# Gate/up products of three dense layers: high and low tokens in one product of 512 columns

## The chip, the cores and the metric

One core of a Trainium2 chip. The time is device microseconds of one execution. The kernel before takes 2243.74 us, the median of 3 runs (2243.52 to 2244.27).

## What is computed

One batch of 256 tokens, width 1,024, goes through four layers in fp32. Layers 0 and 1 are a first block (attention, a layer norm, a feed-forward part; layer 1's is a mixture of 8 experts), layers 2 and 3 a second one (a gated delta rule beside a local attention, then a feed-forward part with a convolution over the tokens). The change touches the feed-forward part of layers 0, 2 and 3:

```python
def swiglu(x, w_gate, w_up, w_down):            # layer 0, inner width 3584
    return (jax.nn.silu(x @ w_gate) * (x @ w_up)) @ w_down
# layers 2 and 3, inner width 2816: h = x @ ffn_up is convolved over the tokens (3 taps and a bias,
# per channel), its gate half goes through gelu, is multiplied by the other half, then @ ffn_down
```

## The kernel before

Every matrix product is done in three products of rounded numbers (type fp32r): a weight w is split into w_hi (w rounded) and w_lo = w - w_hi, and the tokens in the same way. `mm3` (line 787) then adds hi*hi, hi*lo and lo*hi into one PSUM bank.

**Weights.** They come in units of 128x2048 (1 MB), in the order of `stream_order`. SP loads them into six slots `raw`, one after the other. `split_hi` (line 519) on the scalar engine casts a unit into one of three places `w_hi`; `split_lo` (line 529) on the vector engine subtracts into `w_lo`. The unit that goes into a place waits until the products that read the place before have ended. `walk(key)` (through `ahead`, line 535) stands in both engines' programs and splits the unit three behind `key`. All orders are written out by hand, in each engine's own queue.

**A dense stage** (`dense_ffn`, line 986) has n steps: 14 in layer 0, 11 in layers 2 and 3. A step s makes 256 gate and 256 up channels. `gate_up(s)` reads two units, the first and the last four of the eight 128-row chunks of x. For each unit, each half (gate, up), each m (128 channels of the half) and each chunk kc there are three products: weights 128x128 stationary, 256 tokens moving, out 128x256. Gate fills bank 4 + 2 (s % 2), up the bank after it, so the steps take turns with two pairs of banks. `down(s)` multiplies the hidden tile of the step with unit ("dn", s) into banks 0 to 3: 24 products of 512 columns. The order on the matmul engine is

```
gate_up(0), then for s = 0 .. n-4: gate_up(s+1), down(s)
then gate_up(n-2), gate_up(n-1), down(n-3),
then for each tile of tokens t: down(n-2, t), down(n-1, t)
```

`down(s)` waits for `hidden` of s, the last operation of `split_hidden` (line 2116: a cast and a subtraction, both 128x512, on the vector engine).

**Behind a step.** Layer 0: the scalar engine takes silu of the gate bank (line 1544), the vector engine multiplies with the up bank (line 2081) and splits the result. Layers 2 and 3: for each half the scalar engine writes the last tap and the bias from the bank (line 1556, two instructions of 128x256), then the vector engine adds the other two taps, again from the bank (lines 2096 and 2101, two instructions each). Then gelu (`gelu`, line 1565), the product with the up half (`gated_mul`, line 2110) and `split_hidden`. The scalar queue of a step is: split for walk("gu", s, 0), the taps of both halves, split for walk("gu", s, 1), gelu, split for walk("dn", s-1). The vector queue is: split, convolution of gate, convolution of up, split, multiply, hidden split, split.

`features` (line 826) makes these products and also those of the input projections of layers 2 and 3. `open_bank` (line 750) waits on the matmul engine until the reader of a bank's former contents is done.

Of the kernel before, what the change touches and what calls it, by code (L numbers as in the profile page):

```python
# [28 lines left out]
P = 128  # L29
S = 256  # L30
# [196 lines left out]
def build_program(nc, A, plan, debug=None):  # L227
    cst_np, cst_at = constants()
    NC = cst_np.shape[1]
    with ExitStack() as ctx:  # L230
# [65 lines left out]
        local_tmp = arena[:, 1024:1536].rearrange("p (a b c) -> p a b c", a=4, b=16)  # L296
        ffn = carve(0, [("sg", (2, 2, S)), ("cbg", (2, 2, S)), ("cbv", (2, 2, S)), ("gg", (2, 2, S)), ("h", (2, 2, S))])
        moe = carve(0, [("sel", (NT, P)), ("lgT", (S,)), ("more", (NT, NE, NE)), ("even", (NT, NE, NE)), ("sg", (2, 512)),
# [450 lines left out]
        def _(pe):  # L749
# [75 lines left out]

            def features(o, key_a, key_b, cols, name_a, names_b, units=range(2), stage=None):

                for i, key in ((i, (key_a, key_b)[i]) for i in units):
                    if stage:
                        for t in range(NT):  # L830
                            tile_ready(stage, t, (i,))
                    u = unit(M, pe, key)
                    for half in range(2):
                        for m in range(2):
                            for kc in range(4 * i, 4 * i + 4):
                                c0 = (kc % 4) * 512 + cols(half, m)
                                mm = mm3(o[half][:, m * S:(m + 1) * S], [w[:, c0:c0 + P] for w in u],
                                         [a[:, kc, :] for a in xT], kc == 0 and m == 0, kc == KC - 1, lone=False)
                        if i == 1:
                            mm.then_inc(*M.groups.mark(*names_b[half]))  # L840
                    if i == 0:
                        mm.then_inc(*M.groups.mark(*name_a))
                        released(M, unit_at[key], *name_a)
                    else:
                        released(M, unit_at[key], *names_b[1])
# [140 lines left out]
            def dense_ffn(L):  # L986
                n = FFN_STEPS[L]

                def gate_up(s):
                    o = [open_bank(M, 4 + 2 * (s % 2) + half) for half in range(2)]  # L990
                    features(o, ("gu", L, s, 0), ("gu", L, s, 1), lambda half, m: half * 256 + m * P,
                             ("unit", "gu", L, s, 0), [("gu", L, s, 0), ("gu", L, s, 1)],
                             stage=None if s else (L, "mix"))

# [132 lines left out]
            def delta(L):  # L1127
# [20 lines left out]
                def project(nb, b0, units=range(2)):  # L1148
                    features([bank[b0 + j] for j in range(2)], ("in", L, 2 * nb), ("in", L, 2 * nb + 1),
                             lambda j, m: (2 * j + m) * P, ("unit", "in", L, 2 * nb),  # L1150
                             [("cv", L, 2 * nb), ("cv", L, 2 * nb + 1)], units)
# [237 lines left out]
        def _(ac):  # L1389
# [135 lines left out]
            def half_squares(L, which, t, halves):  # L1525
# [7 lines left out]
                root(L, which, t, ss[:, t, 0:1], 1.0 / DM, C("rms_eps"))  # L1533

            def dense_act(L):
                n = FFN_STEPS[L]
                for s in range(n):
                    b = 4 + 2 * (s % 2)
                    walk("gu", L, s, 0)
                    if L == 0:  # L1540
                        ac.wait_ge(*M.groups.at("gu", L, s, 0))
                        if s >= 2:
                            ac.wait_ge(*hidden.at(L, s - 2))
                        nc.scalar.activation(ffn["sg"][:, s % 2, :, :].rearrange("p a b -> p (a b)"), bank[b][:, :], ACT.Silu) \
                            .then_inc(*M.free[b].mark("sg", L, s))
                        walk("gu", L, s, 1)
# [18 lines left out]
            def gelu(L, s):  # L1565
                ac.wait_ge(*M.free[4 + 2 * (s % 2)].at("cb", L, s, 0))
                nc.scalar.activation(ffn["gg"][:, s % 2, :, :].rearrange("p a b -> p (a b)"),
# [296 lines left out]
        def _(ve):  # L1864
# [197 lines left out]
            def pre_turned(L, which, t):  # L2062
# [3 lines left out]
                for g in range(2):  # L2066
# [4 lines left out]
                        .then_inc(*M.free[b].mark("xT", (L, which), t, g))  # L2071

            def dense_dve(L):
                n = FFN_STEPS[L]
                for s in range(n):
                    b = 4 + 2 * (s % 2)
                    walk("gu", L, s, 0)
                    if L == 0:
                        ve.wait_ge(*M.free[b].at("sg", L, s))
                        ve.wait_ge(*M.groups.at("gu", L, s, 1))  # L2080
                        V_.tensor_tensor(ffn["h"][:, s % 2, :, :].rearrange("p a b -> p (a b)"),
                                         ffn["sg"][:, s % 2, :, :].rearrange("p a b -> p (a b)"), bank[b + 1][:, :], ALU.mult) \
                            .then_inc(*M.free[b + 1].mark("h", L, s))
                        walk("gu", L, s, 1)
                        ve.wait_ge(*M.free[b + 1].at("h", L, s))
                        split_hidden(L, s)
# [3 lines left out]
                    for half, buf in enumerate((ffn["cbg"], ffn["cbv"])):  # L2090
                        ve.wait_ge(*M.groups.at("gu", L, s, half))
                        ve.wait_ge(*M.act.at("tap", L, s, half))
                        o = bank[b + half]
                        for m in range(2):
                            c = half * 22 + 2 * s + m
                            step(V_.scalar_tensor_tensor(buf[:, s % 2, m, 1:S], o[:, m * S:m * S + S - 1], fcw[:, c, 1:2],
                                                         buf[:, s % 2, m, 1:S], ALU.mult, ALU.add))
                        sync()
                        for m in range(2):
                            c = half * 22 + 2 * s + m  # L2100
                            ins = V_.scalar_tensor_tensor(buf[:, s % 2, m, 2:S], o[:, m * S:m * S + S - 2], fcw[:, c, 0:1],
                                                          buf[:, s % 2, m, 2:S], ALU.mult, ALU.add)
                        ins.then_inc(*M.free[b + half].mark("cb", L, s, half))
                    walk("gu", L, s, 1)
# [5 lines left out]
            def gated_mul(L, s):  # L2110
                ve.wait_ge(*M.act.at("gelu", L, s))
                ve.wait_ge(*M.free[5 + 2 * (s % 2)].at("cb", L, s, 1))
                chain(V_.tensor_tensor(ffn["h"][:, s % 2, :, :], ffn["gg"][:, s % 2, :, :], ffn["cbv"][:, s % 2, :, :], ALU.mult))
# [610 lines left out]
```

## Time and profile before

| | |
|---|---|
| median of 3 runs | 2243.74 us |
| profiled execution | 2243.76 us, span of its trace 2242.0 us |
| matmul engine (PE) busy | 2177.8 us, 97%, 12,316 products |
| weight loads (PEld) busy | 1864.8 us, 83% |
| vector engine (DVE) busy | 1699.2 us, 76% |
| scalar engine (ACT) busy | 1389.8 us, 62% |
| mean granted clock | 0.992 of full |

PE is the matmul engine, PEld its weight loads, which run beside products. The length of a product includes its way through the pipeline, so products overlap in the rows: what one costs is the distance to the start of the next. "[0.91 <-ACT ...]" is idle time ahead of an instruction and what ended it. L790 is the one line in `mm3` that issues every product of the three-product kind.

### The profile page before, as it was taken

Reading aid. Unit: us, or ns where it says so; the run is one execution under the profiler, and the core shown is the slowest. Engines: PE = TensorE matmul, PEld = TensorE weight load, DVE = VectorE, ACT = ScalarE, POOL = GpSimd, SP = SyncE. Lnnn points to the kernel's source line nnn. Section 1 sums busy time; section 2 is a strip of 40 time slices with the busy share of each in tenths; the row PEclk is TensorE's granted clock in tenths of the full one; section 3 lists DMA queues with packets and bytes.
Section 4 is the critical chain, followed back from the end, with each engine's and each line's share of the span. In section 5 each row is a group of like instructions: output and inputs, shape, how many; then the busy total and the mean of one; then the engine's idle time right before and its main releaser. Section 6 shows DMA issues by size and latency. Waiting matters only on the chain.

```text
span 2242.0 us, 32331 instructions
## 1 busy us (share of the span) xinstructions
PE 2177.8 (97%) x12316; PEld 1864.8 (83%) x12316; DVE 1699.2 (76%) x1876; ACT 1389.8 (62%) x1470; POOL 54.9 (2%) x72
## 2 busy tenths in 40 slices
PE   8899999889999999999999999989999999999998
PEld 6699997668888888888888887769979998988998
DVE  6745457768888888888888889867677777776766
ACT  5543334747777777777777777656465446565444
POOL 2000000010000000000000003000000000000000
PEclk9999999999999999999999999999999999999999
DMA  9655555359999999999999999844135554233551
GB/s 385 230 196 184 185 182 183 117 181 384 369 388 374 382 374 379 378 374 383 367 386 369 392 360 393 338 157 151 66 124 206 178 188 146 93 123 141 180 190 55
DMA packets 82234, 573.35 MB, mean 256 GB/s; under 512 B 9603, under 2 KB 9715, under 8 KB 16803
## 3 DMA queue, kind: packets, MB, share of 16 engines
q1 hardware_dynamic: 76752, 545.82, 64.4%
q0 software_dynamic: 5376, 26.12, 3.2%
q8 instruction: 70, 1.15, 0.2%
q14 instruction: 36, 0.27, 0.0%
HBM read 564.03 MB, written 17.83 MB: 260 GB/s over the span
## 4 chain that ended last, share of the span: by engine, by line
PE 86%; ACT 5%; DVE 5%; issue 2%; DMA 1%; SPq 0%; ACTq 0%; POOL 0%; DVEq 0%
PE bank L790 79%; ACT w_hi L527 2%; DVE w_lo L532 2%; PE bank L1095 1%; ACT arena L1430 1%; PE bank L1220 1%; PE bank L1230 1%; PE bank L1135 1%; DVE R L1937 0%; ACT L527 0%; PE bank L872 0%; PE bank L864 0%; DMA raw<-in_wu_qkv 0%; DVE arena L1950 0%; PE bank L765 0%
## 5 line engine op out<-in xcount | busy, mean ns | idle before, releaser
L532 DVE TENSOR_TENSOR w_lo<-raw,w_hi 128x2048 fp32r<-128x2048 f32 x506 | 1159.1, 2301 | 348.9 <-ACT w_hi L527 347.3
L527 ACT CAST w_hi<-raw 128x2048 fp32r<-128x2048 f32 x506 | 965.7, 1911 | 456.3 <-PE bank L790 453.6
L790 PE MATMUL bank<-w_hi,xT_hi 128*128 128x512 f32 x1184 | 472.4, 399 | 16.0 <-DVE w_lo L532 5.4
L790 PE MATMUL bank<-w_hi,xT_lo 128*128 128x512 f32 x1184 | 464.5, 392 | 0.0
L790 PE MATMUL bank<-w_lo,xT_hi 128*128 128x512 f32 x1184 | 464.1, 392 | 0.0
L790 PE MATMUL bank<-xT_hi,w_hi 128*128 128x256 f32 x1344 | 381.5, 284 | 7.1 <-DVE w_lo L532 3.9
L790 PE MATMUL bank<-xT_lo,w_hi 128*128 128x256 f32 x1344 | 381.0, 283 | 0.0
L790 PE MATMUL bank<-xT_hi,w_lo 128*128 128x256 f32 x1344 | 381.0, 283 | 0.0
L790 PE MATMUL bank<-w_hi,aT_hi 128*128 128x512 f32 x864 | 343.8, 398 | 3.2 <-DVE w_lo L532 3.2
L790 PE MATMUL bank<-w_lo,aT_hi 128*128 128x512 f32 x864 | 336.9, 390 | 0.0
L790 PE MATMUL bank<-w_hi,aT_lo 128*128 128x512 f32 x864 | 336.8, 390 | 0.0
L790 PEld LDWEIGHTS bank<-w_hi,xT_hi 128*128 128x128 f32 x1184 | 224.0, 189 | 75.5 <-DVE w_lo L532 13.8
L790 PEld LDWEIGHTS bank<-xT_hi,w_hi 128*128 128x128 f32 x1344 | 258.5, 192 | 8.9 <-issue 7.7
L790 PEld LDWEIGHTS bank<-w_hi,xT_lo 128*128 128x128 f32 x1184 | 224.0, 189 | 48.2
L790 PEld LDWEIGHTS bank<-w_lo,xT_hi 128*128 128x128 f32 x1184 | 224.5, 190 | 44.4 <-issue 0.2
L790 PEld LDWEIGHTS bank<-xT_lo,w_hi 128*128 128x128 f32 x1344 | 258.6, 192 | 1.1
L790 PEld LDWEIGHTS bank<-xT_hi,w_lo 128*128 128x128 f32 x1344 | 258.6, 192 | 0.0
L790 PEld LDWEIGHTS bank<-w_hi,aT_hi 128*128 128x128 f32 x864 | 162.4, 188 | 37.4 <-DVE w_lo L532 4.8
L790 PEld LDWEIGHTS bank<-w_hi,aT_lo 128*128 128x128 f32 x864 | 162.2, 188 | 35.1
L790 PEld LDWEIGHTS bank<-w_lo,aT_hi 128*128 128x128 f32 x864 | 162.6, 188 | 30.4
L1556 ACT ACTIVATE arena<-bank,fcw 128x256 f32<-128x256 f32 x88 | 44.9, 560 | 61.3 <-PE bank L790 61.3
L1592 ACT ACTIVATE arena<-bank 128x512 f32<-128x512 f32 x56 | 33.6, 600 | 42.7 <-PE bank L790 42.6
(334 smaller groups left out, 1610.1 us busy)
## 6 DMA issues: line engine op xcount, KB each, us to landing
raw<-in_wu_eg SPq DMA_DIRECT2D x112, 1024.0 KB, 7.0
raw<-in_wu_eu SPq DMA_DIRECT2D x112, 1024.0 KB, 7.1
raw<-in_wu_ed SPq DMA_DIRECT2D x112, 1024.0 KB, 7.3
raw<-in_wu_up SPq DMA_DIRECT2D x44, 1024.0 KB, 4.8
raw<-in_wu_ffn_gu SPq DMA_DIRECT2D x28, 1024.0 KB, 4.9
raw<-in_wu_in SPq DMA_DIRECT2D x28, 1024.0 KB, 4.8
raw<-in_wu_down SPq DMA_DIRECT2D x22, 1024.0 KB, 4.9
raw<-in_wu_ffn_d SPq DMA_DIRECT2D x14, 1024.0 KB, 4.9
```

The costliest lines, as they stand in the source:

```text
L527: nc.scalar.copy(w_hi[:, place(i), :], src).then_inc(*E.hi.mark("unit", i))
L532: nc.vector.tensor_tensor(w_lo[:, place(i), :], raw[:, i % RAW, :], w_hi[:, place(i), :].bitcast(F32), ALU.subtract) \
L790: mm = nc.tensor.matmul(o, l[i], r[j], start=(first and n == 0), stop=(last and n == 2), skip_group_check=not lone)
L1095: mm = nc.tensor.transpose(o[:, c * P:(c + 1) * P], moe["h"][:, f % 2, c * P:(c + 1) * P], ident)
L1135: return lambda dst, h: nc.tensor.matmul(dst, lhs(h), rhs(h), start=True, stop=True)
L1220: of_level(n, "X", t, t, lambda dst, i: nc.tensor.matmul(dst, dn["LT"][:, i, :], dn["D"][:, i, :], start=True, stop=True))
L1230: of_level(n, "D", t, 2 + t, lambda dst, i: nc.tensor.matmul(dst, dn["DT"][:, i, :], dn["Xl"][:, i, :], start=True, stop=True))
L1430: ins = nc.scalar.activation(att["pr"][:, i, e, a:b], att["s"][:, i, e, a:b], ACT.Exp, bias=nmax[:, i, e, q:q + 1], scale=-1.0, accum_out= ...
L1556: ins = nc.scalar.activation(buf[:, s % 2, m, :], bank[b + half][:, m * S:(m + 1) * S], ACT.Identity, bias=fcw[:, c, 3:4], scale=fcw[:, c, ...
L1592: nc.scalar.activation(moe["sg"][:, f % 2, :], bank[b][:, :], ACT.Silu).then_inc(*E.free[b].mark(tag, "sg", f))
```

## The change

The high and low parts of x^T become one tensor, the parts 8 KB apart in a partition. `features` of the dense layers now makes two products for a chunk where it made three: w_hi stationary with 512 moving columns (256 high, 256 low) into a whole bank, and w_lo with the 256 high columns into the second half of the same bank. Each (half, m) has a bank of its own, 4 + 2 half + m, so a step fills four banks, and every step the same four. The first half of a bank then holds hi*hi, the second the corrections; they are added afterwards: the scalar engine copies the second half to SBUF (`corrections`), the vector engine adds it to the first (`sum_half`), and everything behind reads the sum from SBUF. The input projections keep the old function under the name `features_in`. The order of steps, units and splits stays.

```diff
-        xT = [sb(f"xT_{part}", [P, KC, S], F32R) for part in ("hi", "lo")]
+        x_both = sb("xT", [P, 2, KC, S], F32R)
+        xT = [x_both[:, part, :, :] for part in range(2)]
...
+            def features(L, s, stage=None):
+
+                for i in range(2):
+                    key = ("gu", L, s, i)
...
+                    u = unit(M, pe, key)
+                    for half in range(2):
+                        for m in range(2):
+                            b = 4 + 2 * half + m
+                            o = open_bank(M, b) if i == 0 else bank[b]
+                            both = o[:, :].rearrange("p (a n) -> p a n", a=2)
+                            for kc in range(4 * i, 4 * i + 4):
+                                c0 = (kc % 4) * 512 + half * 256 + m * P
+                                nc.tensor.matmul(both, u[0][:, c0:c0 + P], x_both[:, :, kc, :], start=(kc == 0), stop=False,
+                                                 skip_group_check=True)
+                                mm = nc.tensor.matmul(o[:, S:2 * S], u[1][:, c0:c0 + P], xT[0][:, kc, :], start=False,
+                                                      stop=(kc == KC - 1), skip_group_check=True)
+                        if i == 1:
+                            mm.then_inc(*M.groups.mark("gu", L, s, half))
...
+            def corrections(L, s, half):
+                ac.wait_ge(*M.groups.at("gu", L, s, half))
+                if s:
+                    for m in range(2):
+                        ac.wait_ge(*M.free[4 + 2 * half + m].at("sum", L, s - 1))
+                for m in range(2):
+                    ins = nc.scalar.copy(ffn["cor"][:, half, m, :], bank[4 + 2 * half + m][:, S:2 * S])
+                ins.then_inc(*M.act.mark("cor", L, s, half))
+
+            def summed(L, s, half):
+                for m in range(2):
+                    ac.wait_ge(*M.free[4 + 2 * half + m].at("sum", L, s))
...
                     if L == 0:
-                        ac.wait_ge(*M.groups.at("gu", L, s, 0))
+                        corrections(L, s, 0)
+                        corrections(L, s, 1)
+                        summed(L, s, 0)
...
                     for half, buf in enumerate((ffn["cbg"], ffn["cbv"])):
-                        ac.wait_ge(*M.groups.at("gu", L, s, half))
+                        corrections(L, s, half)
+                        summed(L, s, half)
                         for m in range(2):
                             c = half * 22 + 2 * s + m
-                            ins = nc.scalar.activation(buf[:, s % 2, m, :], bank[b + half][:, m * S:(m + 1) * S], ACT.Identity,
+                            ins = nc.scalar.activation(buf[:, s % 2, m, :], ffn["sum"][:, half, m, :], ACT.Identity,
...
+            def sum_half(L, s, half):
+                ve.wait_ge(*M.groups.at("gu", L, s, half))
+                ve.wait_ge(*M.act.at("cor", L, s, half))
+                for m in range(2):
+                    b = 4 + 2 * half + m
+                    V_.tensor_tensor(ffn["sum"][:, half, m, :], bank[b][:, 0:S], ffn["cor"][:, half, m, :], ALU.add) \
+                        .then_inc(*M.free[b].mark("sum", L, s))
...
                     for half, buf in enumerate((ffn["cbg"], ffn["cbv"])):
-                        ve.wait_ge(*M.groups.at("gu", L, s, half))
+                        sum_half(L, s, half)
                         ve.wait_ge(*M.act.at("tap", L, s, half))
-                        o = bank[b + half]
+                        o = ffn["sum"][:, half, :, :]
```

In layer 0 the vector engine runs `sum_half` for both halves and then multiplies silu by the second sum.

## Rows read from the trace of the kernel before

**Rows 1.** The page: busy time of each engine, and the chain by engine and line.

```profile
PE 2177.8 (97%) x12316; PEld 1864.8 (83%) x12316; DVE 1699.2 (76%) x1876; ACT 1389.8 (62%) x1470; POOL 54.9 (2%) x72
...
PE 86%; ACT 5%; DVE 5%; issue 2%; DMA 1%; SPq 0%; ACTq 0%; POOL 0%; DVEq 0%
PE bank L790 79%; ACT w_hi L527 2%; DVE w_lo L532 2%; PE bank L1095 1%; ACT arena L1430 1%; PE bank L1220 1%; PE bank L1230 1%; PE bank L1135 1%; DVE R L1937 0%; ACT L527 0%; PE bank L872 0%; PE bank L864 0%; DMA raw<-in_wu_qkv 0%; DVE arena L1950 0%; PE bank L765 0%
```

**Rows 2.** Busy time in the stretches of the three dense stages; columns: stretch, length, busy (count) per engine, granted clock, DMA share, GB/s.

```profile
107.00:346.00 239.00, 239.00 (x1681) 225.63 (x1681) 126.01 (x94) 89.57 (x59) 0.00 (x0) 0.99 0.53 190
1677.00:1864.50 187.50, 186.92 (x1321) 176.46 (x1322) 135.85 (x166) 94.84 (x101) 0.00 (x0) 1.00 0.53 186
2049.00:2236.00 187.00, 186.97 (x1320) 176.15 (x1320) 132.85 (x162) 91.03 (x96) 0.00 (x0) 1.00 0.42 150
```

**Rows 3.** Order of time on PE, one step of layer 2; columns: start, length, engine, line, operation.

```profile
1700.69 0.40 PE L790 MATMUL bank<-w_hi,aT_hi 128*128 128x512 f32 x1
1700.92 0.40 PE L790 MATMUL bank<-w_lo,aT_hi 128*128 128x512 f32 x1
...
1705.93 0.39 PE L790 MATMUL bank<-w_hi,aT_lo 128*128 128x512 f32 x1
1706.15 0.28 PE L790 MATMUL bank<-xT_hi,w_hi 128*128 128x256 f32 x1
1706.27 0.28 PE L790 MATMUL bank<-xT_lo,w_hi 128*128 128x256 f32 x1
...
1717.67 0.40 PE L790 MATMUL bank<-w_hi,aT_hi 128*128 128x512 f32 x1
```

**Rows 4.** Groups of instructions, shapes apart; columns: name, shapes, count, busy us, mean ns, idle before.

```profile
L790 PE MATMUL bank<-xT_hi,w_hi 128*128 128x256 f32 x1344 | 381.5, 284 | 7.1 <-DVE w_lo L532 3.9 <-DVE xT_lo L1894 3.2
...
L2096 DVE SCALAR_TENSOR_TENSOR arena<-bank,fcw,arena 128x255 f32<-128x255 f32 x88 | 38.3, 477 | 20.0 <-ACT arena L1556 19.9
L2212 DVE TENSOR_TENSOR arena<-arena,bank 128x512 f32<-128x512 f32 x56 | 38.1, 681 | 0.0
...
L2113 DVE TENSOR_TENSOR arena<-arena 128x512 f32<-128x512 f32 x22 | 15.1, 684 | 0.0
...
L1956 DVE TENSOR_TENSOR aT_lo<-bank,aT_hi 128x256 fp32r<-128x256 f32 x24 | 10.1, 421 | 11.0 <-ACT aT_hi L1446 10.9
...
L1446 ACT CAST aT_hi<-bank 128x256 fp32r<-128x256 f32 x24 | 8.9, 370 | 10.4 <-PE bank L874 10.4
```

**Rows 5.** Order of time on PEld: weight loads of one-column products.

```profile
1536.85 1.87 PEld L1145 LDWEIGHTS bank<-cst,arena 128*128 128x128 f32 x16
```

**Rows 6.** Order of time around the last step of layer 2: DVE, then ACT, then PE.

```profile
1844.48 2.29 DVE L532 TENSOR_TENSOR w_lo<-raw,w_hi 128x2048 fp32r<-128x2048 f32 x1 [0.82 <-ACT w_hi L527]
1846.69 0.87 DVE L2096 SCALAR_TENSOR_TENSOR arena<-bank,fcw,arena 128x255 f32<-128x255 f32 x2
...
1849.37 0.87 DVE L2096 SCALAR_TENSOR_TENSOR arena<-bank,fcw,arena 128x255 f32<-128x255 f32 x2 [0.91 <-ACT arena L1556]
...
1851.10 2.29 DVE L532 TENSOR_TENSOR w_lo<-raw,w_hi 128x2048 fp32r<-128x2048 f32 x1
...
1854.49 0.69 DVE L2122 TENSOR_TENSOR aT_lo<-arena,aT_hi 128x512 fp32r<-128x512 f32 x1
...
1845.43 1.02 ACT L1556 ACTIVATE arena<-bank,fcw 128x256 f32<-128x256 f32 x2 [0.98 <-PE bank L790]
...
1856.23 0.39 PE L790 MATMUL bank<-w_hi,aT_hi 128*128 128x512 f32 x1
```

**Rows 7.** A stretch at half clock (columns as rows 2), and PE starts behind idle time.

```profile
107.60:111.00 3.40, 3.40 (x18) 3.40 (x18) 3.40 (x2) 0.00 (x0) 0.00 (x0) 0.50 0.93 347
...
1452.50:1455.80 3.30, 3.30 (x5) 1.35 (x4) 0.60 (x1) 0.00 (x0) 2.28 (x2) 0.50 0.31 72
...
106.76 0.36 PE L790 MATMUL bank<-xT_hi,w_hi 128*128 128x256 f32 x1 [3.92 <-DVE w_lo L532]
...
1451.14 1.10 PE L1295 MATMUL bank<-raw,arena 128*128 128x512 f32 x2 [3.35 <-issue]
```

More of the change, by code:

```diff
@@ L831, in features, with features_in @@
                             tile_ready(stage, t, (i,))
+                    u = unit(M, pe, key)
[12 more added lines that the diff above has]
+                            mm.then_inc(*M.groups.mark("gu", L, s, half))
+                    name = ("gu", L, s, 1) if i else ("unit", "gu", L, s, 0)
+                    if i == 0:
+                        mm.then_inc(*M.groups.mark(*name))
+                    released(M, unit_at[key], *name)
+            def features_in(o, key_a, key_b, cols, name_a, names_b, units=range(2)):
+                for i, key in ((i, (key_a, key_b)[i]) for i in units):
                     u = unit(M, pe, key)
@@ L989, in gate_up @@
                 def gate_up(s):
[L990 to L993, printed above, removed]
+                    features(L, s, None if s else (L, "mix"))
                 def down(s, tiles=range(NT)):
@@ L1148, in project @@
                 def project(nb, b0, units=range(2)):
-                    features([bank[b0 + j] for j in range(2)], ("in", L, 2 * nb), ("in", L, 2 * nb + 1),
+                    features_in([bank[b0 + j] for j in range(2)], ("in", L, 2 * nb), ("in", L, 2 * nb + 1),
                              lambda j, m: (2 * j + m) * P, ("unit", "in", L, 2 * nb),
@@ L1540, in dense_act @@
                     if L == 0:
-                        ac.wait_ge(*M.groups.at("gu", L, s, 0))
+                        corrections(L, s, 0)
+                        corrections(L, s, 1)
+                        summed(L, s, 0)
                         if s >= 2:
                             ac.wait_ge(*hidden.at(L, s - 2))
-                        nc.scalar.activation(ffn["sg"][:, s % 2, :, :].rearrange("p a b -> p (a b)"), bank[b][:, :], ACT.Silu) \
-                            .then_inc(*M.free[b].mark("sg", L, s))
+                        nc.scalar.activation(ffn["sg"][:, s % 2, :, :], ffn["sum"][:, 0, :, :], ACT.Silu).then_inc(*M.act.mark("sg", L, s))
                         walk("gu", L, s, 1)
@@ L1565, in gelu @@
             def gelu(L, s):
-                ac.wait_ge(*M.free[4 + 2 * (s % 2)].at("cb", L, s, 0))
+                ac.wait_ge(*M.dve.at("cb", L, s, 0))
                 nc.scalar.activation(ffn["gg"][:, s % 2, :, :].rearrange("p a b -> p (a b)"),
@@ L2078, in dense_dve @@
                     if L == 0:
[L2079 to L2083, printed above, removed]
+                        sum_half(L, s, 0)
+                        sum_half(L, s, 1)
+                        for m in range(2):
+                            ve.wait_ge(*M.free[6 + m].at("sum", L, s))
+                        ve.wait_ge(*M.act.at("sg", L, s))
+                        V_.tensor_tensor(ffn["h"][:, s % 2, :, :], ffn["sg"][:, s % 2, :, :], ffn["sum"][:, 1, :, :], ALU.mult) \
+                            .then_inc(*M.dve.mark("h", L, s))
                         walk("gu", L, s, 1)
-                        ve.wait_ge(*M.free[b + 1].at("h", L, s))
+                        ve.wait_ge(*M.dve.at("h", L, s))
                         split_hidden(L, s)
@@ L2100, in dense_dve @@
                             c = half * 22 + 2 * s + m
-                            ins = V_.scalar_tensor_tensor(buf[:, s % 2, m, 2:S], o[:, m * S:m * S + S - 2], fcw[:, c, 0:1],
+                            ins = V_.scalar_tensor_tensor(buf[:, s % 2, m, 2:S], o[:, m, 0:S - 2], fcw[:, c, 0:1],
                                                           buf[:, s % 2, m, 2:S], ALU.mult, ALU.add)
-                        ins.then_inc(*M.free[b + half].mark("cb", L, s, half))
+                        ins.then_inc(*M.dve.mark("cb", L, s, half))
                     walk("gu", L, s, 1)
@@ L2111, in gated_mul @@
                 ve.wait_ge(*M.act.at("gelu", L, s))
-                ve.wait_ge(*M.free[5 + 2 * (s % 2)].at("cb", L, s, 1))
+                ve.wait_ge(*M.dve.at("cb", L, s, 1))
                 chain(V_.tensor_tensor(ffn["h"][:, s % 2, :, :], ffn["gg"][:, s % 2, :, :], ffn["cbv"][:, s % 2, :, :], ALU.mult))
```

7 lines of the change are left out of this document (3 added, 4 removed).

## The prediction

> **What bounds the kernel now.** I read the page first. The matmul engine is busy 97% of the span, and the chain that ended last lies on it for 86%, of which 79% on the one line that issues every three-product group [rows 1]. Then the three dense stages, each as one stretch: matmul engine busy 239.00 of 239.00 us, 186.92 of 187.50 and 186.97 of 187.00, vector engine 53 to 73%, scalar engine 37 to 51%, DMA 53% or less [rows 2]. So inside a dense stage nothing but the stream of products sets the time; the other engines count only where something they make is late.
>
> Then the stream of one step of layer 2 [rows 3]. The down product of the step before starts at 1700.69, the gate/up products at 1706.15, the next down at 1717.67. 24 products of 512 columns take 5.46 us (0.227 each), 96 of 256 columns take 11.52 us (0.120 each). At the full clock, 2.4 GHz, 512 and 256 columns are 0.2133 and 0.1067 us of streaming. Both kinds carry 0.0133 us more than their columns.
>
> **What the change removes on the matmul engine.** A triple (one K chunk, one 128-column block of weights) was 3 × 256 columns = 0.360 us. It becomes 512 + 256, the same 768 columns in two products: 0.227 + 0.120 = 0.347 us, 0.0133 less. There are 36 steps (14 + 11 + 11) of 32 triples, 1,152 of the 1,344 high-high products of that kind in the page [rows 4]; the other 192 belong to the projections, which keep the old function. 1,152 × 0.0133 = 15.4 us: 6.0 in layer 0 and 4.7 in each of layers 2 and 3. No trace row alternates the two sizes. Where they meet, the product behind the switch from 512 to 256 comes 0.12 after the first, and the first 512 behind a 256 lasts 0.23 to 0.24 [rows 3], so a pair lies between 0.346 and 0.349: 16.1 to 12.7 us in all. Could the weight load be the limit of the 256-column product? Sixteen loads with one-column products take 1.87 us, (1.87 - 0.19) / 15 = 0.112 us apart [rows 5], under 0.120, so no load holds the pair back. I take 15.4.
>
> By the Trainium skill ("TensorE: Matmul & The Clock Gate", Back-to-back issue gap) a warm product costs N/2.4 plus about 2.5 ns, isolated. By that fixed cost the removed products would give 1,152 × 2.5 ns = 2.9 us. This trace disagrees, with 13.3 ns at both sizes.
>
> **What it adds on the scalar and vector engines.** Per step four scalar copies of 128x256 out of a bank and four vector adds of 128x256. The nearest rows are a 128x256 cast from a bank, 0.370 us, and a 128x256 vector operation that reads a bank, 0.421 [rows 4]; back to back a vector pair takes about 0.77. Bounds: the copy up to 0.56, as the scaled reads of a bank have it (1.02 a pair [rows 6]); the add up to 0.48, as the convolution's operations [rows 4]. Below these ends nothing bears. Layer 0 then carries some 1.4 us more of vector and 1.2 of scalar work a step beside 16.5 us of products: its hidden tile goes through one chain (two copies, two adds, silu, multiply) whose last part used to wait for the same second half. It ends within 1 us of where it did, behind 8.2 us of down products, so I cost it at zero.
>
> In layers 2 and 3 the convolution alternates: copy, add, then the tap on the scalar engine, which can only start behind the add, then the vector engine again. Before, each tap pair ran while the vector engine still split weights. Now the vector engine does per half 0.77 of adds, then stands while a tap pair (1.02) and two hand-overs (about 0.1 each) pass: 2.0 us per half, less the 0.91 that it already stood ahead of the second half [rows 6]. So the hidden tile of a step comes 3.1 us later. In the middle steps this is free: a down product of 5.46 us and a whole gate_up of 11.1 lie between a step and the use of its hidden tile. Weights of the unit that is split behind the taps come 3 us later too, with about 2 us to spare.
>
> The last steps have no such cover. gate_up(9) and gate_up(10) follow each other without a down product, so the vector engine enters step 10 late: 3.1, plus 0.4 as the gate_up is shorter, less the 0.82 and little more that it stood idle there = 2.4 us. Step 10 adds its own 3.1. The hidden tile of step 10 moves by 5.5 us against the product stream. Before, it was ready at 1854.49 + 0.69 = 1855.18 and the product that needs it started at 1856.23 [rows 6], 1.05 us of slack. The new stall is 5.5 - 1.05 = 4.5 us, once in each of layers 2 and 3. Bounds: with shorter hand-overs 4.0, with adds of 0.48 5.2.
>
> **Banks.** Every step now opens all four banks 4 to 7, where steps used to take turns with two. With a down product between (5.46) they are long free. Not in the two back-to-back pairs of a layer: the third bank is wanted 2.8 us into the next gate_up, and its add lands about 3.0 after the last product, by the order add, tap, convolution, add. I take 0.25 us a pair, 0.5 a layer (0 to 1.2); what is queued behind the waiting product is the rest of the gate_up. In layer 0 the add lands at about 1.2 us: no wait.
>
> **The clock.** An idle matmul engine loses more than its idle time here. After 3.92 us of idle the granted clock was 0.50 from 107.60 to 111.00, the 1.2 GHz level, and 18 products started in 3.40 us where 28 would have; it also read 0.50 from 1452.50, behind 3.35 us of idle that ended at 1451.14 [rows 7]. A stall of 4.5 us is longer than both. The price is 10 × 0.120 = 1.2 us with 256 columns; with 512 an estimate of 1.6 (8 products of 0.427 in 3.4 us against 15). I take 1.5 a layer; bounds 0 and 3.
>
> Moved or removed otherwise: weight splits keep their place in each queue, no DMA is added or moved, and SP's loads wait on the same splits. The convolution reads its rows from SBUF now. Vector operations of 128x512 take 684 ns with SBUF sources only and 681 with a bank among them [rows 4], so nothing is booked. The Trainium skill ("Perfetto Trace Analysis", Optimizing Scalar/DVE Operations) has the vector engine's access at about 60 ns on SBUF and 125 on PSUM. By it the eight convolution operations of a step would save 0.5 us and the stalls shrink by about 1 us over both layers; these rows don't show it.
>
> **Sum.** Layer 0: -6.0. Layers 2 and 3, each: -4.7 + 4.5 + 0.5 + 1.5 = +1.8. Together -6.0 + 3.6 = -2.4. The profiled execution took 2243.76 us around its span of 2242.0, the median is 2243.74, so both bases agree: 2241.4 us.
>
> **Rivals.** 1. The stalls come, the clock stays up or the stalls come out near 4 us. For: a fall at an idle stretch depends on more than its length, and 36 products are ahead of the stall at full speed. Against: both idle stretches of this size shown above were followed by a fall. Time 2241.4 - 3.0 = 2238.4.
> 2. The tails don't stall: the scalar engine reaches the copies so early that the adds fill vector idle time. Against: the vector engine stood only 0.82 + 0.91 us in the whole last step before. Time 2243.7 - 15.4 = 2228.3.
> 3. Slower: the vector engine becomes the bound of every step of layers 2 and 3. A step there has three splits (6.6), the convolution (3.5), adds (1.5), multiply and hidden split (1.8) and two stands for the taps (2.4): 15.8 of 16.55 us. It decides from 0.75 us a step on, which needs the adds near 0.6 apart or the hand-overs near 0.3. At adds of 0.61 apart (1.0 more a step) the excess is about 0.3 a step over 16 steps, 5 us, the tails grow to 6 each and the bank waits to 2: 2243.7 - 15.4 + 5 + 12 + 4 + 3 = 2252. Against it: a 256-element add at 0.42.
> 4. Slower as well: the 0.0133 doesn't go with the product, since a 256-column product behind a 512-column one, or the moving side in two pieces 8 KB apart, costs the difference. With only 2.5 ns saved a triple it is 2243.7 - 2.9 + 2 × (4.3 + 0.3 + 1.5) = 2253. This is also what the page's fixed cost would make of it. Against: row for row the excess is the same at both sizes.
>
> **How the numbers follow.** Forecast 0.50; rival 1 0.20; rival 2 0.08; rival 3 0.13; rival 4 0.09. What a measurement can tell here is 0.2%, 4.5 us, so faster means under 2239.2, slower over 2248.2. Faster: rival 2, two thirds of rival 1 and a little of the forecast's low side, 0.26. Slower: rivals 3 and 4 but for their mild ends, and the forecast's top, 0.20. Same: 0.54. The range leaves out rival 2 and the far half of 3 and 4: 2236 to 2250.
>
> **What would show it.** Gate/up triples 0.347 apart in the new trace (0.358 would be rival 4). A wait of matmuls for the vector engine's hidden low part of 4 to 5 us ahead of the last step's down product in layers 2 and 3 and none in layer 0; waits of 0.2 to 0.4 for adds one step after the first and at the last; a granted clock of 0.50 right behind each tail stall. In middle steps, waits of matmuls for splits or adds would mean rival 3. Without tail stalls the forecast is wrong on the high side by up to 13 us.

## The result and the profile after the change

The changed kernel takes 2249.53 us (median of 8 runs, 2245.49 to 2251.06) against 2243.80 (8 runs of the kernel before, 2243.52 to 2246.16). The ratio is 1.0023, with an interval of 1.0012 to 1.0034: 5.7 us slower. The forecast was 2241.4, 2.4 us faster than before. The time lies inside the range of 2236 to 2250, on the other side of no change.

The page of the profiled execution, whose span is 2243.7 us. It is the fastest of the eight (2245.49 us), so stages are compared with each other below, not whole spans. Busy time by engine, then the chain by line:

```profile
PE 2171.5 (97%) x11164; PEld 1802.8 (80%) x11164; DVE 1749.2 (78%) x2020; ACT 1432.7 (64%) x1614; POOL 55.9 (2%) x72
...
PE bank L792 60%; PE bank L843 11%; PE bank L845 6%; ACT w_hi L529 2%; DVE w_lo L534 2%; PE bank L1117 1%; ACT arena L1452 1%; PE bank L1242 1%; PE bank L1252 1%; PE bank L1157 1%; DVE R L1974 0%; ACT L529 0%; PE bank L897 0%; PE bank L889 0%; DVE arena L1987 0%
```

Beside [rows 1] the matmul engine has 1,152 products fewer, as intended, but is only 6.3 us less busy (2177.8 to 2171.5). The vector engine has 50.0 us more work and the scalar engine 42.9. The products that were on one line are now on three: L792 for all the old forms, L843 for the products of 512 columns and L845 for those of 256.

The three dense stages of the changed kernel, with the columns of [rows 2], which they answer:

```profile
105.00:346.00 241.00, 240.94 (x1249) 204.02 (x1250) 150.24 (x156) 107.99 (x118) 0.53 (x1) 0.99 0.52 188
1669.00:1861.00 192.00, 186.22 (x969) 158.06 (x969) 151.87 (x209) 108.27 (x143) 0.00 (x0) 0.99 0.50 181
2040.00:2236.00 196.00, 190.21 (x985) 159.98 (x984) 153.59 (x217) 107.81 (x145) 0.00 (x0) 0.99 0.39 142
```

In layer 0 (first row) the matmul engine is still busy throughout. In layers 2 and 3 it now stands for 5.8 us of each stretch, where it stood 0.6 and 0.0 before; 1.5 of the 5.8 lie at the start of the stage, which the stretches of [rows 2] mostly leave out. The waits of the matmul engine in layer 2 and layer 3 (1660 to 1870 and 2040 to 2240) say for what; columns: what waited, for whom, sum, times, longest:

```profile
PE bank L792 <- DVE aT_lo L2169: 4.2, 1, 4.2
PE bank L792 <- DVE xT L1931: 1.8, 1, 1.8
PE bank L843 <- DVE xT L1931: 1.5, 1, 1.5
```

The first line is the low part of the last step's hidden tile, 4.2 us once in layer 2. Layer 3 has the same line. The second is the start of the next layer's input projection, the third the start of this feed-forward stage; the kernel before has both as well. No wait for a split or an add in a middle step is in either list, and layer 0 has no wait at all between 107 and 346.

The products of one middle step of layer 2, in order of time; columns as [rows 3]:

```profile
1693.54 0.40 PE L843 MATMUL bank<-xT,w_hi 128*128 128x512 f32 x1
1693.77 0.28 PE L845 MATMUL bank<-xT,w_lo 128*128 128x256 f32 x1
1693.88 0.40 PE L792 MATMUL bank<-w_hi,aT_hi 128*128 128x512 f32 x1
...
1699.12 0.39 PE L792 MATMUL bank<-w_hi,aT_lo 128*128 128x512 f32 x1
1699.35 0.39 PE L843 MATMUL bank<-xT,w_hi 128*128 128x512 f32 x1
1699.58 0.28 PE L845 MATMUL bank<-xT,w_lo 128*128 128x256 f32 x1
1699.69 0.40 PE L843 MATMUL bank<-xT,w_hi 128*128 128x512 f32 x1
...
1710.52 0.28 PE L845 MATMUL bank<-xT,w_lo 128*128 128x256 f32 x1
1710.64 0.40 PE L792 MATMUL bank<-w_hi,aT_hi 128*128 128x512 f32 x1
```

The first gate/up product starts at 1699.35 and the down product behind the last at 1710.64: 11.29 us for 32 pairs, 0.353 a pair. Before, the 96 products took 11.52 [rows 3], over all steps 11.51. So a step gains 0.22 us where the forecast had 0.43. Inside a pair the row of 256 follows 0.23 to 0.24 behind the row of 512, and the next 512 follows 0.11 to 0.12 behind that.

The end of layer 2 in the changed kernel, the vector engine, then the scalar engine, then the matmul engine, answering [rows 6]:

```profile
1840.60 0.75 DVE L2115 TENSOR_TENSOR arena<-bank,arena 128x256 f32<-128x256 f32 x2
1842.57 0.88 DVE L2143 SCALAR_TENSOR_TENSOR arena<-arena,fcw 128x255 f32<-128x255 f32 x2 [1.22 <-ACT arena L1593]
...
1844.28 0.75 DVE L2115 TENSOR_TENSOR arena<-bank,arena 128x256 f32<-128x256 f32 x2
1846.25 0.88 DVE L2143 SCALAR_TENSOR_TENSOR arena<-arena,fcw 128x255 f32<-128x255 f32 x2 [1.22 <-ACT arena L1593]
1847.17 0.88 DVE L2148 SCALAR_TENSOR_TENSOR arena<-arena,fcw 128x254 f32<-128x254 f32 x2
1848.05 2.29 DVE L534 TENSOR_TENSOR w_lo<-raw,w_hi 128x2048 fp32r<-128x2048 f32 x1
...
1851.44 0.69 DVE L2169 TENSOR_TENSOR aT_lo<-arena,aT_hi 128x512 fp32r<-128x512 f32 x1
```

```profile
1845.13 1.09 ACT L1593 ACTIVATE arena<-arena,fcw 128x256 f32<-128x256 f32 x2 [2.06 <-DVE arena L2115]
```

```profile
1847.65 0.39 PE L792 MATMUL bank<-w_hi,aT_lo 128*128 128x512 f32 x1
1852.28 0.47 PE L792 MATMUL bank<-w_hi,aT_hi 128*128 128x512 f32 x1 [4.24 <-DVE aT_lo L2169]
...
1853.56 0.63 PE L792 MATMUL bank<-w_lo,aT_hi 128*128 128x512 f32 x1
1853.98 0.63 PE L792 MATMUL bank<-w_hi,aT_lo 128*128 128x512 f32 x1
1854.41 0.63 PE L792 MATMUL bank<-w_hi,aT_hi 128*128 128x512 f32 x1
```

Per half the vector engine adds for 0.75 us and then stands 1.22 us for the tap of 1.09. The hidden low part is done at 1852.13 (1851.44 + 0.69), the matmul engine has stood since 1848.04 (1847.65 + 0.39) and starts at 1852.28. Against the stream of products the tile comes 12.4 us behind the end of the last gate_up (1839.69); before it was 7.1 (1855.18 against 1848.05). Behind the stall it runs at half clock: products of 512 columns start 0.43 us apart, and in the stretch the granted clock reads 0.50 (the 1.2 GHz level), as in [rows 7]:

```profile
1852.90:1856.30 3.40, 3.40 (x10) 2.66 (x9) 2.13 (x2) 0.69 (x2) 0.00 (x0) 0.50 0.67 234
```

**By stages.** From the starts of the products, before and after: the first gate/up product of layer 0 to the end of its last gate_up 222.88 and 220.25 us (-2.6); layer 2 170.47 and 168.58 (-1.9); layer 3 170.47 and 168.52 (-1.95). From the end of the gate_ups to the next projection in layer 2: 48.81 and 54.96 (+6.15). To the end of the span in layer 3: 22.5 and 28.6 (+6.1). Together that is +5.8, the difference of the medians +5.7. The profiled execution shows less of it because its first dense stage starts at 105.06, not at 106.76, and 2.1 us are gained between the end of layer 0 and the start of layer 2. The change touches nothing there; the clock differs. From 28 to 34 us the granted clock reads 0.72 before and 1.00 after, and between the two layers the stretches at 0.50 add up to 23.9 us before and 20.5 after.

### The profile page after: what moved, and what is told of

The parts are those of the page before. It is cut to its first block, busy times and chain, and to the rows that moved or that the text cites. A ratio compares the mean times of both kernels' runs of the same rounds, so it can differ in the third digit from the quotient of the medians.

```text
span 2243.7 us, 30455 instructions
## 1 busy us (share of the span) xinstructions
PE 2171.5 (97%) x11164; PEld 1802.8 (80%) x11164; DVE 1749.2 (78%) x2020; ACT 1432.7 (64%) x1614; POOL 55.9 (2%) x72
## 4 chain that ended last, share of the span: by engine, by line
PE 85%; DVE 6%; ACT 6%; issue 2%; DMA 1%; SPq 0%; ACTq 0%; POOL 0%; DVEq 0%
PE bank L792 60%; PE bank L843 11%; PE bank L845 6%; ACT w_hi L529 2%; DVE w_lo L534 2%; PE bank L1117 1%; ACT arena L1452 1%; PE bank L1242 1%; PE bank L1252 1%; PE bank L1157 1%; DVE R L1974 0%; ACT L529 0%; PE bank L897 0%; PE bank L889 0%; DVE arena L1987 0%
## 5 line engine op out<-in xcount | busy, mean ns | idle before, releaser
L792 PE MATMUL bank<-w_hi,xT 128*128 128x512 f32 x2368 | 756.9, 394 | 15.5 <-DVE w_lo L534 5.4
L792 PEld LDWEIGHTS bank<-w_hi,xT 128*128 128x128 f32 x2368 | 446.7, 189 | 122.2 <-DVE w_lo L534 14.5
L792 PE MATMUL bank<-w_lo,xT 128*128 128x512 f32 x1184 | 462.9, 391 | 0.0
L843 PE MATMUL bank<-xT,w_hi 128*128 128x512 f32 x1152 | 409.8, 400 | 7.0 <-DVE w_lo L534 4.0
L792 PE MATMUL bank<-w_hi,aT_hi 128*128 128x512 f32 x864 | 345.9, 400 | 11.9 <-DVE aT_lo L2169 8.5
L792 PE MATMUL bank<-w_hi,aT_lo 128*128 128x512 f32 x864 | 338.5, 392 | 0.0
L792 PE MATMUL bank<-w_lo,aT_hi 128*128 128x512 f32 x864 | 338.0, 391 | 0.0
L845 PE MATMUL bank<-xT,w_lo 128*128 128x256 f32 x1152 | 324.1, 281 | 0.0
L843 PEld LDWEIGHTS bank<-xT,w_hi 128*128 128x128 f32 x1152 | 217.2, 189 | 61.9 <-issue 4.2
L792 PEld LDWEIGHTS bank<-w_lo,xT 128*128 128x128 f32 x1184 | 223.6, 189 | 44.1 <-issue 0.2
L845 PEld LDWEIGHTS bank<-xT,w_lo 128*128 128x128 f32 x1152 | 218.2, 189 | 1.1
L792 PEld LDWEIGHTS bank<-w_hi,aT_hi 128*128 128x128 f32 x864 | 162.9, 188 | 48.3 <-issue 12.6
L792 PEld LDWEIGHTS bank<-w_hi,aT_lo 128*128 128x128 f32 x864 | 163.0, 189 | 36.0
L792 PEld LDWEIGHTS bank<-w_lo,aT_hi 128*128 128x128 f32 x864 | 163.4, 189 | 31.1
L792 PE MATMUL bank<-xT,w_hi 128*128 128x256 f32 x384 | 69.8, 284 | 0.0
L2115 DVE TENSOR_TENSOR arena<-bank,arena 128x256 f32<-128x256 f32 x144 | 53.9, 416 | 20.2 <-ACT arena L1563 20.2
```

What stands on the lines that cost most here:

```text
L792: mm = nc.tensor.matmul(o, l[i], r[j], start=(first and n == 0), stop=(last and n == 2), skip_group_check=not lone)
L843: nc.tensor.matmul(both, u[0][:, c0:c0 + P], x_both[:, :, kc, :], start=(kc == 0), stop=False, skip_group_check=True)
L845: mm = nc.tensor.matmul(o[:, S:2 * S], u[1][:, c0:c0 + P], xT[0][:, kc, :], start=False, stop=(kc == KC - 1), skip_group_check=True)
L2115: V_.tensor_tensor(ffn["sum"][:, half, m, :], bank[b][:, 0:S], ffn["cor"][:, half, m, :], ALU.add) \
```

## The experiments

The rival causes after the result were, for the short gain per pair: alternation of lengths (A), the moving side in two pieces (B), the second product into the bank of the first (C); for the rest, how much of the loss hangs on the tails. Kernels measured together share the runs of the kernel before: l0only, warm and tail3 go with a median of 2243.97 us (18 runs), the last four below with 2244.50 (24 runs). Differences are taken from these.

**micro**: nothing but streams of products with a fresh 128x128 weight tile each, one pattern after another. `M` is the matmul, `two` the moving side in two pieces, `one` in one piece. It is one execution, and the granted clock reads 1.00 in every stretch used below (the list is shortened from the code):

```
M(one, 512) x96 | M(two, 512) x96 | M(256) x160
[M(two, 512) -> bank b, M(256) -> bank b] x80          # as the change has it
[M(one, 512) -> bank b, M(256) -> bank b] x80
[M(two, 512) -> bank b, M(256) -> bank b+4] x80
[4 x M(two, 512), 4 x M(256)] x20 | [16 x M(two, 512), 16 x M(256)] x5
M(one, 384) x160 | [M(one, 384), M(one, 320)] x80
```

> Only streams of products are left of the reference's work, each on a line of its own, at full clock. In the changed kernel a 512-column product that stands directly behind a 256-column one takes 236 to 241 ns to the next start and the pair 353 ns, where 227 + 120 = 347 was forecast. Theory A (the alternation of lengths costs it): every alternating stream shows pairs of 352 to 354, whether the moving side lies in one piece or two and whether the second product goes to the same bank or another; two-piece 512 alone shows 227; groups of four and four show pairs near 350, of sixteen and sixteen near 348; equal 384-column products show 173. Rival B (the moving side in two pieces 8 KB apart): two-piece 512 alone is already 233 or more and the one-piece alternation gives 347. Rival C (the second product adds into the half bank that the first has just written): only the stream into another bank gives 347.

Order of time on the matmul engine, where each uniform pattern is one row (start, length, count):

```profile
42.80 21.92 PE L70 MATMUL bank<-y_one,w_hi 128*128 128x512 f32 x96
64.56 21.92 PE L72 MATMUL bank<-x_two,w_hi 128*128 128x512 f32 x96
86.32 19.36 PE L74 MATMUL bank<-x_two,w_hi 128*128 128x256 f32 x160
105.51 0.40 PE L76 MATMUL bank<-x_two,w_hi 128*128 128x512 f32 x1
105.74 0.28 PE L77 MATMUL bank<-x_two,w_lo 128*128 128x256 f32 x1
105.86 0.40 PE L76 MATMUL bank<-x_two,w_hi 128*128 128x512 f32 x1
...
133.78 0.40 PE L79 MATMUL bank<-y_one,w_hi 128*128 128x512 f32 x1
...
162.04 0.40 PE L82 MATMUL bank<-x_two,w_hi 128*128 128x512 f32 x1
...
190.31 0.63 PE L86 MATMUL bank<-x_two,w_hi 128*128 128x512 f32 x2
...
218.38 1.32 PE L91 MATMUL bank<-x_two,w_hi 128*128 128x512 f32 x5
...
246.21 27.90 PE L95 MATMUL bank<-y_one,w_hi 128*128 128x384 f32 x160
```

The starts divide into prices. 512 columns in one piece and in two pieces both take (64.56 - 42.80) / 96 = 0.2267 us, so B is out. 256 columns alone take (105.51 - 86.32) / 160 = 0.1199. Alternating, a pair takes (133.78 - 105.51) / 80 = 0.3534, with the moving side in one piece 0.3533, with the second product in another bank 0.3534: C is out too. The two add up to 0.3466, so the alternation costs 6.8 ns a pair. In groups of four (from 190.31) a pair takes 0.3509, in groups of sixteen (from 218.38) 0.3479. Read by order, from a 512 behind a 256 to the next start it is 236 ns in place of 227, and the 256 behind it gives back 3. With 384 and 320 columns in turn the pair takes 0.3223, 2.3 ns above 0.3200, what both lengths would take at 13.3 ns above their columns (measured for 384, assumed for 320). So A holds: the loss goes with the changes of length, and 1,152 pairs × 6.8 ns are 7.8 us of the forecast's 15.4. In these pairs the stationary side changes between w_hi and w_lo too, but that isn't it: the down products of the kernel before take w_hi, w_lo, w_hi in turn at one length and stay at 0.227 each, and its gate/up products do so at 0.120. Why a change of length costs time is not shown.

**l0only**: the change in layer 0 alone; layers 2 and 3 run the old three products, taps and convolution out of the bank.

```
 def features(L, s, stage=None):
+    if L > 0:
+        o = [open_bank(M, 4 + 2 * (s % 2) + half) for half in range(2)]
+        features_in(o, ("gu", L, s, 0), ("gu", L, s, 1), ...)     # shortened; three products of 256
+        return
```

> The change in layer 0 alone; layers 2 and 3 as before. Theory (no stall in layer 0, 0.22 us less a step): 14 x 0.22 = 3.1 us faster than before, about 2240.7, and no wait of the matmul engine for a hidden tile. Rival (the changed steps themselves, not the tails of layers 2 and 3, made the loss): no faster than before, 2244 or more.

Measured 2242.41 us (11 runs, 2237.97 to 2243.44), ratio 0.999 (0.9981 to 0.9999). A gain of about 1.6 us where the pair price asks for 3.1 (14 × 0.22). No wait for a hidden tile is in its trace. Layer 0 gains and the loss is in layers 2 and 3; half of the expected gain isn't in the median (see what stays open).

**tail3**: the last two steps of layers 2 and 3 the old way, all others as changed. Same edit as above with another condition:

```
+    if L and s >= FFN_STEPS[L] - 2:
```

> The changed kernel, but the last two steps of layers 2 and 3 in three products of 256 columns, half banks and taps read from the bank, as before. Theory (the loss lies in those tails alone): the two stalls of 4.24 us and the half clock behind them go, 32 steps keep 0.22 us each: 7.0 us less than before, about 2236.8. Where the bank waits of the last pair or a later hidden tile leave something, 2238 to 2240. Rival (the longer drain costs in every step of layers 2 and 3): the time stays near the changed kernel, 2246 or more.

Measured 2239.47 us (8 runs, 2234.37 to 2240.79), ratio 0.9976 (0.9966 to 0.9987): 4.5 us faster than before, where the changed kernel is 5.7 slower, so 10.2 between them. The waits of its matmul engine from 1660 to 1870 (the line L767 is the start of the stage behind the layer):

```profile
PE bank L792 <- DVE xT L1943: 1.8, 1, 1.8
PE bank L767 <- DVE R L2109: 1.6, 1, 1.6
PE bank L848 <- DVE xT L1943: 1.5, 1, 1.5
```

The wait for the hidden low part is gone, and with it the half clock behind it: two stalls of 4.24 and two clock losses of 1.9, 12.3 us, and four steps lose their 0.22 each again, 0.9 us. That makes 11.4 expected, of which 10.2 came.

**warm**: keeps the matmul engine at work in the stall with products on a constant, ahead of the last step's first down product.

```
 for s in (n - 2, n - 1):
+    if L and t == 0 and s == n - 1:
+        keep_warm(9, 4)
     down(s, (t,))
```

> The changed kernel with nine products of the identity into bank 4 (already read) ahead of the last step's first down product in layers 2 and 3, in the time in which the matmul engine stood 4.24 us. Theory (the stalls cost 4.24 us each, and the half clock that follows 1.9 more each): the stalls stay, the half clock behind them goes, 3.8 us less than the changed kernel's median 2249.5, so about 2245.7, and its runs lie closer together. Rival (the clock plays no part, the spread comes from elsewhere): 2249.5 as before, or more by what the nine products take beyond the stall.

Measured 2254.84 us (2251.01 to 2255.03), ratio 1.0041 (1.0028 to 1.0055). A miss, and its trace says why:

```profile
1852.41 7.88 PE L785 MATMUL bank<-cst 128*128 128x512 f32 x18
1859.73 0.80 PE L792 MATMUL bank<-w_hi,aT_hi 128*128 128x512 f32 x1
```

`keep_warm(9, 4)` makes 18 products, two of 0.43 us for each count of its first argument. They hold the engine from 1852.41 to 1859.73, while the hidden low part is done at 1856.82, so they outlast the stall by some 2.8 us in each layer. The time therefore says nothing of the clock's share; warm4 has the right size. Behind the 18 products the granted clock reads 1.00 in both layers (1859.8 to 1863.2 and 2238.5 to 2241.9).

**warm4**: the same with `keep_warm(4, 4)`, some 3.5 us, inside the stall.

> As the run with nine products of the identity, which took 7.3 us (two of 0.43 us each) and so outlasted the stall; now four, 3.5 us, inside the 4.24 us stall. Theory (stall 4.24 us plus 1.9 us of half clock, twice): no half clock directly behind the stalls, 3.8 us less than the changed kernel: 2245.7. Rival (a stretch at half clock turns up elsewhere instead, or the stalls' clock loss isn't what it was in other executions): 2248 to 2250.

Measured 2246.71 us (11 runs, 2244.50 to 2249.66), ratio 1.0009 (1.0 to 1.0018): 2.2 us slower than before in place of 5.7, so 3.5 are back, where 3.8 (2 × 1.9) was the clock's part. The intervals of the two ratios overlap (1.0 to 1.0018 here, 1.0012 to 1.0034 for the changed kernel), so the 3.5 is a rough figure; the trace is the firmer evidence. In layer 2 the last step's down still waits, now as a remainder, from the end of the eight products at 1857.33 to 1858.11, and the stretch behind that wait reads full clock:

```profile
PE bank L792 <- DVE aT_lo L2171: 0.8, 1, 0.8
```

```profile
1858.30:1861.70 3.40, 3.40 (x16) 2.77 (x16) 2.56 (x2) 1.23 (x4) 0.00 (x0) 1.00 0.78 270
```

Layer 3 has the same: a wait of 0.83 and no stretch at 0.50 until 2243.3, behind the layer's last down product. So the fall of the clock behind the tail can be avoided without making the hidden tile any earlier; of the stall itself nothing is gained.

**grouped**: per half and unit, eight products of 512 columns, then eight of 256, in place of 512 and 256 in turn.

```
-    for m in range(2): for kc in chunks: M(both, w_hi, x_both); M(low half, w_lo, xT_hi)
+    for m in range(2): for kc in chunks: M(both, w_hi, x_both)
+    for m in range(2): for kc in chunks: M(low half, w_lo, xT_hi)
```

> The changed kernel, but the eight 512-column products of a half in a unit come first and its eight 256-column products behind them. Theory (each change from 256 to 512 columns and back costs about 17 ns a group, however long the group, from 4.2 ns a pair in groups of four and 1.1 in groups of sixteen): pairs of 348.8 in place of 353.4 ns, a step 11.16 in place of 11.29 us, 36 x 0.13 = 4.7 us under the changed kernel, about 2244.8; both tail stalls stay. Rival (the 353 are made by something else in the kernel, such as its bank waits): the step stays 11.29 and the time 2249.5.

Its gate_up(1) of layer 2, which follows gate_up(0) without a down product between, so that its first two groups are longer by waits for the adds:

```profile
1679.86 2.00 PE L844 MATMUL bank<-xT,w_hi 128*128 128x512 f32 x8
1681.70 1.11 PE L849 MATMUL bank<-xT,w_lo 128*128 128x256 f32 x8
...
1685.73 2.00 PE L844 MATMUL bank<-xT,w_hi 128*128 128x512 f32 x8
1687.57 1.12 PE L849 MATMUL bank<-xT,w_lo 128*128 128x256 f32 x8
1688.52 2.00 PE L844 MATMUL bank<-xT,w_hi 128*128 128x512 f32 x8
1690.36 1.12 PE L849 MATMUL bank<-xT,w_lo 128*128 128x256 f32 x8
1691.32 0.40 PE L792 MATMUL bank<-w_hi,aT_hi 128*128 128x512 f32 x1
```

A group of eight pairs takes 2.79 us (1688.52 - 1685.73), 0.349 a pair, and a middle step, with a down product on both sides, 11.15 us: 0.14 less than in turn, as expected. The tail wait is unchanged (4.3 us in layer 2), as it should be. Measured 2247.51 us (11 runs, 2242.27 to 2250.18), ratio 1.001 (1.0001 to 1.0019): 3.0 us slower than before in place of 5.7, 2.7 gained where 36 × 0.14 = 5.0 were due, with an interval that overlaps the changed kernel's. In its trace the stretch at 0.50 at each tail stall lasts 6.8 us, not 3.4, and begins 1.5 us before the stall of layer 2 ends: the last down products take 23.5 us from the end of the gate_ups, 22.5 in the changed kernel. That is 1.0 us a layer.

**tail3g**: both edits together.

> Groups of eight, and the last two steps of layers 2 and 3 in three products as before. Theory: the kernel with the old tails measured 2239.5, 32 steps x 0.13 us less gives 2235.3. Rival (bank waits or later sums eat it): 2238 or more.

Measured 2232.61 us (5 runs, 2228.90 to 2236.99), ratio 0.9948 (0.9934 to 0.9961), 11.9 us faster than the kernel before, and beyond both kernels by more than the intervals. 32 changed steps × 0.36 are 11.5. Its matmul engine waits in layer 2 for nothing but what the kernel before waited for:

```profile
PE bank L792 <- DVE xT L1947: 1.8, 1, 1.8
PE bank L849 <- DVE xT L1947: 1.5, 1, 1.5
```

**tail3g16**: tail3g with sixteen products of 512 and then sixteen of 256 per unit, half as many changes of length.

> As the last, but sixteen 512-column products of a unit first and then sixteen of 256. Theory: 347.8 ns a pair, 11.13 us a step, 2234.2. Rival (the first half of a step is complete 1.8 us later, so the vector engine is late in the pairs of steps without a down product): no better than groups of eight, with waits for hidden tiles or adds.

Measured 2239.67 us (8 runs, 2236.93 to 2240.54), ratio 0.9974 (0.9964 to 0.9985). A middle step takes 11.11 us, 0.04 less than with groups of eight, but the gate half is now complete only 1 us before the up half, and where two gate_ups follow each other the second waits for the adds that free its banks. Waits of the matmul engine in layer 2, then in layer 0:

```profile
PE bank L849 <- DVE arena L2132: 1.9, 2, 1.5
```

```profile
PE bank L849 <- DVE arena L2132: 0.8, 2, 0.4
```

Layer 3 has the same 1.9. These 4.6 us stand against 32 × 0.04 = 1.3 gained. No wait in the trace explains the remaining 3.8 us of the distance between its median and tail3g's; the clock may (see what stays open).

## Why the prediction was wrong

**The failed step: the price of a pair.** The prediction took 0.347 us for 512 + 256 columns, with bounds of 0.346 and 0.349, and so 15.4 us of gain. The pair takes 0.353, outside both bounds. The gain on the stream is 36 × 0.22 = 7.9 us. The sum of the two uniform prices was right to the nanosecond (0.2267 + 0.1199 in micro); what fails is the step from them to the pair, that a length has one price whatever stands in front of it. The rows gave a warning: where the two sizes meet, the prediction itself read 0.23 to 0.24 for the first 512 behind a 256 [rows 3]. With 0.12 for the 256 that is a pair of 0.35 to 0.36, but the prediction wrote 0.349 as its upper bound and took 0.347. In the changed kernel every 512 is the first behind a 256.

**Rival 4** named alternation as a way to lose the 13.3 ns, at a chance of 0.09, but priced it as all or nothing (0.358, 2253 us). The measured gain, 7.9 us, lies between its 2.9 and the forecast's 15.4. Its 2.9 comes from the 2.5 ns that it cites, not from a row. Its other cause, the moving side in two pieces, costs nothing.

**Right: the tails.** A wait of 4 to 5 us for the hidden low part, once in each of layers 2 and 3 and none in layer 0: 4.24 measured, 4.5 forecast. The mechanism is the one that was argued: two steps without a down product between them, the vector engine standing for the tap in each half (1.22 us, the tap of 1.09 and the hand-overs, forecast 1.02 + 0.2), tap and add in turn. The hidden tile moved by 5.3 us against the stream (12.4 less 7.1), forecast 5.5. tail3 takes it away.

**Right: the clock.** 0.50 behind both stalls, 1.9 us a layer (6.15 less 4.24), forecast 1.5. warm4 takes the fall away by itself, and 3.5 of the 3.8 us come back in the medians. The milder half of rival 1, stalls near 4 us, came close; its other half, no fall of the clock, and its time are out. The prediction's price with 256 columns was misread: of the 18 products counted in [rows 7] two had started before the stretch. 16 start in it, which makes 3.4 - 16 × 0.120 = 1.5 us lost, not 1.2. The 1.5 that it took doesn't change by that.

**Right: banks and middle steps.** The two back-to-back gate_ups take 22.78 where two single ones take 22.58, 0.2 a pair or 0.4 a layer; forecast 0.25 and 0.5. The matmul engine's own rows list no such wait, its weight loads do: they wait for the add 0.4 us in the first pair of layer 2 and 0.2 in the last. No middle step waits, so rival 3 (vector engine the bound) and rival 2 (no tail stall) are out. Layer 0 hides its adds altogether, as booked.

**The sum again**, with the measured sizes: layer 0 -14 × 0.22 = -3.1; layers 2 and 3 each -2.4 + 4.2 + 0.4 + 1.9 = +4.1. Together +5.1, where the medians differ by 5.7. Most of the rest is in the stages above: a down tile behind a changed step takes 5.50 us in place of 5.47, some 25 times. The other corrections cancel (4.5 + 0.5 + 1.5 forecast, 4.2 + 0.4 + 1.9 measured), which is luck; the one term, 15.4 to 7.9, moves -2.4 to +5.1 and turns the sign.

**What stays open.** Against the kernel before and the durations in their own traces, the medians of l0only came out 1.5 us too slow, tail3 2.5, grouped about 3 and tail3g16 3.4, while tail3g did not. Stretches at 0.50 of the clock differ between traces, also in stages that no edit touches. Added up over a span they are 37.3 us before, 37.8 after, 40.9 in l0only, 38.9 in tail3, 43.3 in warm, 43.0 in warm4, 40.7 in grouped, 39.7 in tail3g16 and 27.8 in tail3g, and about half of such a time is lost. In warm4 the additional ones lie ahead of layer 2. Between the profiled executions of tail3g16 and tail3g the clock covers some 6 of 9.8 us, the three dense stages 4.3.

Every run has its own mean granted clock, and this settles a good part. Time × mean clock is an estimate of the time at full clock (too low where products don't set the pace; one step of 0.001 in the noted clock is 2.2 us, so it holds to some 2 us). Means over all runs, as differences to the kernel before (2226.2 us for its 42 later runs); "due" is the sum from the traces without the clock's part:

| | due | time × clock |
|---|---|---|
| changed kernel | +1.3 | +2.5 |
| l0only | -3.1 | -3.4 |
| tail3 | -7.0 | -4.9 |
| warm | +6.8 | +9.3 |
| warm4 | +1.3 | +2.8 |
| grouped | -3.5 | -4.9 |
| tail3g | -11.5 | -11.3 |
| tail3g16 | -8.2 | -6.1 |

By this, 2.5 of the 5.7 us are there at full clock and some 3 are the clock's, and the gaps of l0only and grouped are the clock's altogether. tail3, tail3g16 and warm keep 2 to 2.5 us that no row explains, about what the rounding leaves. Why the clock falls more often in some kernels and executions stays open, as does whether the change has a part in it. One gap of 2.40 us ahead of a projection that no edit touches ends at 1490.74 in the changed kernel and is followed by 0.50; before, it ends at 1498.08 and the clock stays at 1.00.

By the Trainium skill ("TensorE: Matmul & The Clock Gate", Back-to-back issue gap) the gap of a single, isolated product of N columns is N/2.4 plus 2.5 ns at full clock. No run here fits that constant: micro, in a stream where each product has fresh weights, has 13.3 ns above the columns at both 256 and 512 in uniform streams, and 23 for a 512 behind a 256.

## What to carry to other kernels

Price a product with the one in front of it: look in the trace for the very order that a change will produce, and when it shows only once, at a seam, take that row and not the average of the uniform stretches. When products of two lengths are needed, issue them in groups, as long as the groups don't delay what frees their banks. When a chain behind the products grows, look at the end of the stage first: a chain hidden by the next step has no cover at the last, and leaving the last steps in the old form gave back more (10 us) than the whole change saves on the stream (7.9).

## What the runs showed of the hardware

Alternating 512 and 256 columns costs 6.8 ns a pair over the uniform prices of 226.7 and 119.9 ns, the same with one or two pieces on the moving side and with one bank or two; in groups of four 4.3 ns a pair, in groups of sixteen 1.3. So a round of groups costs more when they are longer (6.8, then 17, then 21 ns), with most of it reached at four. 384 and 320 columns in turn cost about 2, if 320 alone costs 13.3 ns over its columns. A product whose moving side lies in two pieces 8 KB apart takes the same 226.7 ns as one in a single piece. And a stall of 4.24 us, closed with products on a constant down to 0.8 us, isn't followed by a fall of the clock, where the stall itself is, in layer 2 and in layer 3.
